# Making the low part of each weight unit with an accumulating DMA instead of a GpSimd subtraction

## What is computed

```python
for l in range(DEPTH):                      # 2
    h = rmsnorm(x, mix_norm_g[l])
    x = x + mixing_layer(h, ...)            # w_in, conv, attention, w_out
    h = rmsnorm(x, ffn_norm_g[l])
    x = x + swiglu(h, w_gate[l], w_up[l], w_down[l])
...
h = rmsnorm_2(x, norm_mix[l])               # second block, 1 layer
oa = _gated_deltanet(...)                   # heads of 128, chunks of 64
ob = _chunk_band_attention(qb, kb, vb, band_bias)
x = x + y @ w_o[l]
x = x + _memory_xattn(...)                  # keys and values from mem, 256 rows
x = x + (jax.nn.silu(gate) * up) @ w_down[l]
```

## Time and profile before

| | |
|---|---|
| median of 3 runs | 2835.74 us (2831.58 to 2839.4) |
| the profiled execution | 2838.97 us, span 2837.5 us |
| mean granted TensorE clock | 0.967 |
| TensorE busy | 2664.9 us, 94% |
| VectorE, ScalarE, GpSimd busy | 1138.0, 902.3, 1309.9 us |
| moved by DMA | 216.35 MB, mean 76 GB/s |

### The profile page before, as it was taken

One profiled execution on the slowest core, in us unless ns is written; L12 is line 12 of the kernel. 1 busy time (PEld: TensorE's weight loads), 2 busy tenths in 40 slices (PEclk: granted clock), 3 DMA queues, 4 the chain that ended last, 5 costly groups with the idle time before them and its releaser, 6 DMA issues.

```text
span 2837.5 us, 33156 instructions
## 1 busy us (share of the span) xinstructions
PE 2664.9 (94%) x13048; PEld 2152.2 (76%) x13048; DVE 1138.0 (40%) x2281; ACT 902.3 (32%) x1359; POOL 1309.9 (46%) x1713
## 2 busy tenths in 40 slices
PE   8889999999979999997999999989999997999997
PEld 6767888887758888876777878667768884888886
DVE  6884111127863111258556654323442322311112
ACT  4343322232433222343223222214552333322222
POOL 5533655656336656543312222334325671465664
PEclk9999999999989999999999989989999999999998
DMA  4212223232112232221101000122212331122322
GB/s 149 71 45 75 90 87 114 81 105 80 55 45 89 95 106 90 91 88 45 45 16 45 30 30 30 45 89 90 82 53 89 104 134 45 65 99 95 106 76 80
DMA packets 36619, 216.35 MB, mean 76 GB/s; under 512 B 4080, under 2 KB 5232, under 8 KB 15856
## 3 DMA queue, kind: packets, MB, share of 16 engines
q1 hardware_dynamic: 36464, 214.23, 22.2%
HBM read 212.12 MB, written 2.10 MB: 75 GB/s over the span
## 4 chain that ended last, share of the span: by engine, by line
PE 79%; DVE 12%; POOL 4%; ACT 3%; issue 2%; DMA 1%; SPq 0%; DVEq 0%; POOLq 0%; ACTq 0%
PE PB L1636 61%; PE PB L1674 4%; POOL WL L2641 3%; PE PB L1638 3%; DVE cc L2280 1%; PE PB L1656 1%; PE PB L1648 1%; ACT WH L1895 1%; PE PB L1820 1%; PE PB L1817 1%; PE PB L1851 1%; PE PB L1832 1%; PE PB L1798 1%; DVE NEWT L2161 1%; PE PB L1839 1%
## 5 line engine op out<-in xcount | busy, mean ns | idle before, releaser
L2641 POOL TENSOR_TENSOR WL<-WR,WH 128x256 fp32r<-128x256 f32 (+1 forms) x1572 | 1152.9, 770 | 1024.2 <-ACT WH L1895 1024.1
L1636 PE MATMUL PB<-HH,WH 128*128 128x512 f32 x1992 | 807.0, 405 | 11.2 <-ACT HH L1907 8.8
L1636 PE MATMUL PB<-HL,WH 128*128 128x512 f32 x1992 | 784.7, 394 | 3.4 <-DVE HL L2182 3.3
L1636 PE MATMUL PB<-HH,WL 128*128 128x512 f32 x1992 | 525.9, 399 | 3.4 <-POOL WL L2641 3.4
L1636 PEld LDWEIGHTS PB<-HH,WH 128*128 128x128 f32 x1992 | 378.9, 190 | 104.3 <-issue 16.4
L1895 ACT ACTIVATE WH<-WR 128x2048 fp32r<-128x2048 f32 (+1 forms) x209 | 371.6, 1778 | 262.4 <-PE PB L1636 247.5
L1636 PEld LDWEIGHTS PB<-HL,WH 128*128 128x128 f32 x1992 | 378.3, 190 | 86.6 <-DVE HL L2182 8.9
L1636 PEld LDWEIGHTS PB<-HH,WL 128*128 128x128 f32 x1992 | 367.8, 189 | 83.1 <-issue 8.2
L1636 PE MATMUL PB<-BH,WH 128*128 128x512 f32 (+1 forms) x912 | 355.9, 393 | 23.4 <-ACT BH L1920 21.0
L1636 PE MATMUL PB<-BL,WH 128*128 128x512 f32 (+1 forms) x912 | 355.3, 392 | 2.5 <-DVE BL L2190 1.1
L1636 PEld LDWEIGHTS PB<-BH,WH 128*128 128x128 f32 x912 | 175.0, 192 | 73.7 <-ACT BH L1920 32.3
(11 more groups left out here) (327 smaller groups left out, 2934.6 us busy)
## 6 DMA issues: line engine op xcount, KB each, us to landing
WR<-in_w_gu SPq DMA_DIRECT2D x66, 1024.0 KB, 4.8
WR<-in_w_dn SPq DMA_DIRECT2D x48, 704.0 KB, 4.1
WR<-in_w_in SPq DMA_DIRECT2D x22, 1024.0 KB, 4.9
WR<-in_qkv SPq DMA_DIRECT2D x12, 1024.0 KB, 4.9
WR<-in_w_out SPq DMA_DIRECT2D x8, 1024.0 KB, 4.9
WR<-in_qk SPq DMA_DIRECT2D x8, 1024.0 KB, 5.0
WR<-in_za SPq DMA_DIRECT2D x4, 1024.0 KB, 4.8
WR<-in_ga SPq DMA_DIRECT2D x4, 1024.0 KB, 4.9
```

The source lines that it names most:

```text
L1636: ins = pe.matmul(out[:, 0:n], wt[:, k * cols + j * P:k * cols + (j + 1) * P], x[:, k, 0:n], start=first, stop=last)
L2641: ins = g.tensor_tensor(m.WL[u % 2][:, part], m.WR[u % 2][:, part], f32(m.WH[u % 2][:, part]), ALU.subtract)
```

## The change

GpSimd's subtraction goes. ScalarE, right after rounding WR to WH, waits for that instruction and writes -WH into WL. GpSimd then issues a DMA that adds WR onto WL, so WL becomes WR - WH. The DMA's completion has a semaphore for each buffer (`wlo0`, `wlo1`, 16 a unit), and TensorE and SyncE wait for that one where they waited for `wlo`. The planner's costs change with it: 4.0 us on ScalarE and 7.0 us from there to the low part, and none on GpSimd.

```diff
-    "wload": (), "consts": (), "split": ("A:whi", "G:wlo"), "mm": (), ...
+    "wload": (), "consts": (), "split": ("A:whi", "A:wneg"), "mm": (), ...
+def low_part(u):
+    return f"wlo{u % 2}", 16 * (u // 2 + 1)
 # pass_time
-            t = max(t, c.known(self.at("wlo" if part else "whi", u)), ...)
+            t = max(t, c.known(low_part(u) if part else self.at("whi", u)), ...)
-            ends["A"] = c.run("A", 2.0, t)
-            ends["G"] = c.run("G", 6.3, ends["A"])
+            ends["A"] = c.run("A", 4.0, t)
+            c.when[low_part(key[0])] = ends["A"] + 7.0
 # tensor_program
-                    te.wait_ge(*at("wlo", u))
+                    te.wait_ge(*low_part(u))
 # scalar_program
             a.activation(m.WH[u % 2][:, 0:n], m.WR[u % 2][:, 0:n], ACT.Copy).then_inc(sems["whi"], 1)
+            ae.wait_ge(*at("whi", u))
+            a.activation(m.WL[u % 2][:, 0:n], f32(m.WH[u % 2][:, 0:n]), ACT.Copy, scale=-1.0).then_inc(sems["wneg"], 1)
 # gpsimd_program
-            ge.wait_ge(*at("whi", u))
-            for a in range(0, n, 256):
-                part = slice(a, min(a + 256, n))
-                ins = g.tensor_tensor(m.WL[u % 2][:, part], m.WR[u % 2][:, part], f32(m.WH[u % 2][:, part]), ALU.subtract)
-            ins.then_inc(sems["wlo"], 1)
+            ge.wait_ge(*at("wneg", u))
+            g.dma_start(f32(m.WL[u % 2][:, 0:n]), m.WR[u % 2][:, 0:n], accum_op=ALU.add).then_inc(sems[f"wlo{u % 2}"], 16)
 # sync_program
-            se.wait_ge(*at("wlo", u - 2))
+            se.wait_ge(*low_part(u - 2))
```

More of the change, by code:

```diff
@@ L217 @@
 KINDS = {
-    "wload": (), "consts": (), "split": ("A:whi", "G:wlo"), "mm": (), "memload": (), "bias": ("G:bias",),
+    "wload": (), "consts": (), "split": ("A:whi", "A:wneg"), "mm": (), "memload": (), "bias": ("G:bias",),
     "gain": ("A:hh", "V:hl"), "sq0": ("A:sq0",), "sq": ("A:sq", "V:acc"), "res": ("V:res",),
@@ L418, in pass_time @@
             op, ks, cols = given["op"], given["ks"][start:given["to"]], given["n"] if given["mode"] == "F" else self.units[u][3]
-            t = max(t, c.known(self.at("wlo" if part else "whi", u)), c.known([x for k in ks for x in (op.hi[k], op.lo[k]) if x]))
+            t = max(t, c.known(low_part(u) if part else self.at("whi", u)), c.known([x for k in ks for x in (op.hi[k], op.lo[k]) if x]))
             t = ends["T"] = c.run("T", len(ks) * (1 if part else 2) * cols * 0.000445, t)
@@ L2715, in build @@
         o = order(m)
-        names = ["tile", "vchain", "vec0", "vec1", "con0", "con1", "pos", "w0", "w1", "memt", "out"]
+        names = ["tile", "vchain", "vec0", "vec1", "con0", "con1", "pos", "w0", "w1", "wlo0", "wlo1", "memt", "out"]
         names += [f"x{c}" for c in range(DC)] + [f"bt{i}{j}" for i in range(2) for j in range(2)]
```

## The result

The changed kernel takes 2900.13 us (median of 4 runs, 2895.53 to 2915.51) where the kernel before takes 2833.66 beside it: a ratio of 1.0241, 95% interval 1.02 to 1.0282. It is slower by 2.4%, where the prediction had 0.5% faster: the time lies within the range of 2800 to 2950, which was drawn wide for the rival R1, but on the other side of no change. Its profiled execution has a span of 2898.9 us, 61.4 more than before.

What follows compares the result with a forecast made beforehand. TensorE bounds the kernel (busy 94% of the span), so other engines count only where it waits. Terms -26 + 2.5 + 9 + 2.2 - 2 = -14.3 us took 2838.97 to 2824.7, as a median 2822; range 2800 to 2950.

Steps and rivals of the forecast that it cites:

- R1: Rival, DMA too slow: X above 8.3 us makes each gate/up unit late, at 9.5 us about 2925 us; chance 36%.
- X: Time from issue of the accumulating DMA to its landing, for a 1 MB unit: 7.7 us, between 4.9 and 10.5.
- The Trainium skill's 12 us: Alternative estimate of X from the skill's load time and half rate for reductions, estimated 330 us slower.
- 9.4 us for a DMA of about 0.69 of the size: Down units (704 KB): time left for the DMA before its low part is wanted, so no cost there.
- The cover of 8.3 us: Gate/up units: X may be 8.3 us before TensorE waits; 7.7 fits with 0.6 us to spare.
- Key/value units: Cross-attention units where one buffer's cycle is on the chain: 14.3 us becomes 17.3, three cycles, +9 us.
- The start: Program start: second copy before the first HH +1.9 us, faster VectorE operations on X's first chunks -4, -2 net.
- The attention blocks: Two blocks, VectorE relieved of GpSimd's subtraction: 14.8 us less one added rounding, 12.9 each, -26 us together.
- The waits for qr and VT: TensorE's waits of 4.9 and 4.0 us in each attention block, both claimed to go.
- The wait for SQ: TensorE's 7.2 us wait in each attention block, taken as layer norm latency and claimed to stay.
- R2: Rival, no change: ScalarE's added work eats VectorE's relief, halving the attention gain to -13, total 2834 us; chance 15%.
- Delta rule and bias: Delta rule: five doubled roundings +9.5, VectorE relief 7, sum +2.5 us. Bias tables at 1912 us: later low part, +2.2.

Runs made afterwards that it cites:

- the best version: Accumulating DMA only for w_in units except the program's first four (18 units), GpSimd's subtraction elsewhere as in the kernel before: 2812.04 us, ratio 0.991.
- the experiment on the down units: The changed kernel with GpSimd's subtraction and no second copy for the 48 down units alone: 2865.87 us, ratio 1.0111.

## Why the prediction was wrong

**X, the landing.** Taken as 7.7 us from 2.1 + 2 x 2.8; measured 7.0 for 1 MB in the median, and 6.9 to 7.1 whenever nothing else moves. The sum was 0.7 us too high; no run tells whether it is the second read that it rightly counts. The Trainium skill's 12 us ("DMA: Bandwidth & Descriptors" and "Collectives: The Full Stack") was too much. Its half rate for a reduction agrees with the DMA engines' time, 1.94 times a copy's. Its 6.15 us are for a load issued from GpSimd, and no run here has one; the copy within SBUF that GpSimd issued landed in 4.6.

**The step that failed: "That leaves ... 9.4 us for a DMA of about 0.69 of the size: free as well."** It set a DMA's time alone against the time until its result is wanted. It left out that the buffer must also be refilled in the same two periods, and above all that the two buffers' transfers run at once and slow each other. The refill by itself would have fitted: with transfers at their speed alone, the round was 5.45 + 4.1 + 2 x 1.39 + 0.3 = 12.6 us of 15.0. In the stage it was 17.05, since the accumulation took 8.1 to 8.8 and the load 5.1 to 5.8. Put at nothing, the six down stages cost 20.3 us, 34 together with what they leave to the stages behind.

**The cover of 8.3 us in gate/up.** It holds for most units, with the DMA at 7.0: the first halves of the three gate/up stages lost only 1.6, 1.0 and 1.0 us. The second halves, entered from a down stage, lost 5.4, 5.3 and 7.4 (the chain has a DMA of 9.77 us at 448.04). Rival R1, the DMA too slow, had the right effect with the wrong condition and place: it wanted X above 8.3 in every gate/up unit, while with nothing beside it X was 7.0, single units passed 8.3 beside an instruction fetch, and what decided were transfers side by side, in the down and the key/value units. R1's note that loads may overlap the DMA was the right one. Its sum for 9.5 us has a slip: 2836 + 108 + 5 - 14 is 2935, not 2925; the range isn't touched by it.

**Key/value units.** The right chain, mis-sized: 17.3 us a cycle, measured 21.2, of which 9.9 instead of 5.8 is the load, which runs beside the other buffer's accumulation. From the first rounding to the last low part of that chain it took 2348.3 - 2275.2 = 73.1 us, before 2303.8 - 2254.9 = 48.9: 24.2 of the stage's 31.3, against +9 predicted. A plain copy by DMA gives +12.1 and the accumulation +31.3, so 19.2 us of the stage come from accumulating instead of copying.

**The start.** -2 predicted, from VectorE's relief; the accumulation took 12.89 us beside the program's first loads. Without four DMAs there the block is 7 us shorter.

**The attention blocks.** The 12.9 us a block were right about the mechanism, and in size where the DMA isn't disturbed: -13.0 and -11.5 in the best version. In the changed kernel it was -7.6 and -7.9, since the start took from the first, and the second was entered from a down stage: its chain begins with an accumulation of 10.12 us, and with the down units subtracted it gained 11.9. The waits for qr and VT went from 4.9 and 4.0 us to none and 1.3. The wait for SQ, which was to stay at 7.2, fell to 3.7 in the first block and 5.0 in the second; the prediction had counted nothing for it, so the agreement in size is in part luck. Rival R2, ScalarE eating the gain, is refuted by the kernel without the DMA: -19.2 and -16.6 with every second copy in place.

**Delta rule and bias.** +2.5 and +2.2 predicted, +2.7 and +2.2 in the profile. That is luck in part: the band stage scatters by some 6 us, the line between the two stages moves with the order, and at the bias tables themselves the low part took 6.97 instead of 5.53 us and the table's load ahead of it 8.00 instead of 6.13, together +3.3.

In short: 61.4 us are -15.5 in attention, +41.8 in the feed-forward, +31.3 in the cross-attention, +3.8 elsewhere. Between the forecast of -14.3 and this lie 75.7 us: 41.8 in the feed-forward, put at nothing, 22.3 in the key/value units, 12.3 in attention and start. What isn't settled is where 5 of the 12.0 us come from that stay in gate/up when the down units are subtracted, why an accumulation can be long beside an instruction fetch, and why halves of a unit leave VectorE as slow as before.

## What to carry to other kernels

Moving work from an engine to a DMA puts it in competition with the loads: price the round of a buffer (accumulate, refill, produce) against its periods with the transfers of both buffers in flight, not the single transfer against its first use. An accumulation cost 1.94 times the DMA time of a copy here, so use it only where another engine's relief is on the path and the queues are quiet, here 18 of 209 units. A kernel that leaves the transfer out and one that makes it a plain copy say in two runs how much of a loss is the transfer and how much the accumulating.

## What was not expected of the hardware

An accumulating DMA within SBUF took 5.4 us for 704 KB and 7.0 for 1 MB alone, 8.8 and up to 12.9 beside other transfers, and a 1 MB load beside it went from 4.8 to 9.9 us. How much is beside it counts: for 1 MB accumulations of the changed kernel without an instruction fetch the median is 6.94 us with no load, 6.97 with up to 0.6 MB loaded meanwhile, 7.5 with 0.6 to 0.85 MB and 9.5 with more. Beside a fetch of instructions, of 16 KB at most, it could take as long (up to 9.34 us), as read in the experiment on the down units. With accumulations the DMA engines were 95% busy at 186 GB/s, so here their busy share, not the bandwidth, said that they were full. Issuing an accumulating one took GpSimd 880 ns, a plain copy of the same size 554 ns, as the group of the kernel with the plain copy shows:

```profile
L2646 POOL DMA_DIRECT2D WL<-WR x209 | 115.7, 554 | 1754.6 <-ACT WL L1902 1754.5
```
